# A hybrid layer and a mixture-of-experts block on one core: norms summed earlier and elsewhere, splits moved up, and down weights laid out as 8 KB rows

## The reference

```python
def hybrid_layer(x, ...):                       # block 1
    h = rmsnorm(x, ln1_g)
    z = h @ w_in                                # q, k, v of three attentions, conv input, forget gate, gates
    branches = (sliding_window_gqa, conformer_conv, forgetting_attention, moba_attention)
    merged = sum over branches of sigmoid(gate) * (branch @ w_br)
    x = x + merged @ w_out
    h2 = rmsnorm(x, ln2_g)
    u = causal_depthwise_conv(h2 @ w_up)        # D_FF = 2816
    return x + (silu(g_ff) * v_ff) @ w_down

def reference(...):
    x = rmsnorm(hybrid_layer(x), final_g)       # eps 1e-6
    h = rms_norm(x, attn_norm_g)                # block 2, eps 1e-5
    u_pool, u_q, u_k, u_v = split(h @ w_in_2)
    x = x + concat(multiscale_pool(u_pool), diff_attention(rotary(u_q), rotary(u_k), u_v)) @ w_out
    x = x + cross_attention(rms_norm(x, xattn_norm_g), rms_norm(mem, mem_norm_g), w_cq, w_ckv, w_co)
    x = x + moe_ffn(rms_norm(x, ffn_norm_g))    # 32 experts, top 4, clamped swiglu
    return rms_norm(x, final_norm_g)
```

## Time and profile before

| | before |
|---|---|
| time, median of 3 runs | 1783.1 us (1780.71 to 1783.13) |
| profiled execution | 1782.5 us, span 1780.7 us |
| PE busy | 1624.3 us, 91% of the span |
| DVE busy | 746.3 us, 42% |
| ACT busy | 485.1 us, 27% |
| POOL busy | 155.2 us, 9% |
| moved by DMA | 526.45 MB, mean 296 GB/s |

### The profile page before, as it was taken

One profiled execution on the slowest core, in us unless ns is written; L12 is line 12 of the kernel. 1 busy time (PEld: TensorE's weight loads), 2 busy tenths in 40 slices (PEclk: granted clock), 3 DMA queues, 4 the chain that ended last, 5 costly groups with the idle time before them and its releaser, 6 DMA issues.

```text
span 1780.7 us, 22817 instructions
## 1 busy us (share of the span) xinstructions
PE 1624.3 (91%) x9782; PEld 1030.0 (58%) x9782; DVE 746.3 (42%) x1308; ACT 485.1 (27%) x820; POOL 155.2 (9%) x190
## 2 busy tenths in 40 slices
PE   7899999989999899998999888898989898988885
PEld 6899989989999888985333323232323232323221
DVE  5798765778885567653211111111212121212122
ACT  3445645446554435542100000000101010101001
POOL 1200001403550012010000000000000000000000
PEclk9999999999999899999999999999999999999998
DMA  8564434546665353646899999999999999999995
GB/s 187 166 205 146 131 119 123 173 132 190 190 190 181 122 177 107 230 171 238 356 424 423 422 425 423 424 423 423 424 424 424 424 423 425 424 423 425 424 424 243
DMA packets 210938, 526.45 MB, mean 296 GB/s; under 512 B 18745, under 2 KB 136414, under 8 KB 178062
## 3 DMA queue, kind: packets, MB, share of 16 engines
q1 hardware_dynamic: 207104, 519.34, 75.6%
q0 software_dynamic: 3184, 5.37, 1.6%
q10 hardware_dynamic: 542, 0.21, 0.0%
HBM read 523.24 MB, written 1.61 MB: 295 GB/s over the span
## 4 chain that ended last, share of the span: by engine, by line
PE 56%; DMA 36%; DVE 5%; ACT 2%; issue 1%; SPq 0%; POOL 0%; ACTq 0%; DVEq 0%
PE bank L594 55%; DMA slot_ring<-in_w_down 13%; DMA slot_memx<-in_w_down 8%; DMA slot_late<-in_w_down 5%; DMA slot_high<-in_w_down 4%; DMA slot_late<-in_w_gu 2%; DVE slot_ring_r L1856 1%; DMA slot_last<-in_w_gu 1%; DMA slot_high<-in_w_gu 1%; DMA slot_ring<-in_w_in 1%; PE bank L1105 1%; ACT high_r L1441 0%; DVE rstd L1895 0%; DVE rot_tmp L2256 0%; DVE x_sb L1864 0%
## 5 line engine op out<-in xcount | busy, mean ns | idle before, releaser
L594 PE MATMUL bank<-h_hi_r,high_r 128*128 128x256 f32 x1000 | 286.4, 286 | 3.6 <-DVE h_lo_r L1856 3.6
L1856 DVE TENSOR_TENSOR slot_ring_r<-slot_ring,high_r 128x1024 fp32r<-128x1024 f32 x198 | 244.9, 1279 | 97.4 <-ACT high_r L1441 95.0
L594 PE MATMUL bank<-h_lo_r,high_r 128*128 128x256 f32 x1000 | 284.3, 284 | 0.0
L594 PE MATMUL bank<-h_hi_r,slot_ring_r 128*128 128x256 f32 x952 | 270.4, 284 | 0.0
L1860 DVE TENSOR_SCALAR ga<-bank 128x512 f32<-128x512 f32 x32 | 22.1, 692 | 583.8 <-PE bank L594 583.8
L1441 ACT ACTIVATE high_r<-slot_ring 128x1024 fp32r<-128x1024 f32 x198 | 198.0, 1052 | 73.0 <-PE bank L594 47.0
L594 PEld LDWEIGHTS bank<-h_hi_r,high_r 128*128 128x128 f32 x1000 | 192.1, 192 | 5.6 <-DVE h_lo_r L1856 4.3
L594 PEld LDWEIGHTS bank<-h_lo_r,high_r 128*128 128x128 f32 x1000 | 192.4, 192 | 0.1
L1441 ACT ACTIVATE th_e<-ga 128x512 f32<-128x512 f32 x32 | 20.2, 630 | 619.7 <-DVE ga L1860 619.7
L594 PEld LDWEIGHTS bank<-h_hi_r,slot_ring_r 128*128 128x128 f32 x952 | 183.4, 193 | 0.0
L594 PE MATMUL bank<-slot_ring,xg 128*64 128x512 f32 x528 | 124.3, 603 | 12.1 <-DMA slot_ring<-in_w_gu 12.1
(11 more groups left out here) (413 smaller groups left out, 2925.9 us busy)
## 6 DMA issues: line engine op xcount, KB each, us to landing
slot_ring<-in_w_gu SPq DMA_DIRECT2D x66, 1024.0 KB, 22.1
slot_high<-in_w_gu SPq DMA_DIRECT2D x50, 1024.0 KB, 22.1
slot_ring<-in_w_down SPq DMA_DIRECT2D x49, 1024.0 KB, 22.7
slot_last<-in_w_gu SPq DMA_DIRECT2D x38, 1024.0 KB, 22.2
slot_ring<-in_w_in SPq DMA_DIRECT2D x36, 1024.0 KB, 5.0
slot_late<-in_w_gu SPq DMA_DIRECT2D x32, 1024.0 KB, 22.1
slot_high<-in_w_down SPq DMA_DIRECT2D x25, 1024.0 KB, 23.3
slot_ring<-in_w_up SPq DMA_DIRECT2D x44, 512.0 KB, 4.6
```

The source lines that it names most:

```text
L594: return e.matmul(o, lhs, rhs, start=start, stop=stop, skip_group_check=True)
L1856: return e.tensor_tensor(o, i, j, op)
```

## The change

- **Start.** The first transfer of constants holds ident and ones only. The sums of squares come from x as it lands, token by token: eight DVE operations (128x256, `accum_out`), a reduction, ACT's root of two columns, a reciprocal, and two products with diag(norm) on PE that spread it over the partitions. The eight sums and squares and the wide reciprocal go. The rows are turned in two steps. h is split in halves with unit ub0's lo between them. The product for the bias tables comes after ub0 on PE, their copies after the split that goes with ub1 on DVE. The split of wfc moves ahead of the ub loop on ACT and behind it on DVE.
- **Memory's norm** goes in three steps of three, three and two tiles.
- **ln2, xattn, ffn.** `add_squares`: POOL adds tiles 2 and 3, then 4 and 5, of the squares to tiles 0 and 1; PE sums tiles 0, 1, 6 and 7 only, after the last projection.
- **Border.** The attn_g norm is computed straight from the residual: its squares are scaled by `gain_sq` = sqrt((g1^2 + eps2) / D), eps is eps1 * eps2, the gain is the product `gain12`. The squares for final_g follow on ACT into `x_sq`, POOL adds the eight tiles in three operations after the last rotation, PE needs one call, and DVE applies it between its splits for upool and the pooling. The mark that frees two more slots for SP comes at down's end.
- **Cross attention.** `cross_probs(2)` and `(3)` stand before `round_co(0)` and `(1)` on ACT.
- **Down units.** Partition p takes rows 2p and 2p+1, one row of 8 KB; the transposes read every other hidden column.

```diff
-        MEM_STEPS = ((0, 1), (2, 3), (4, 5), (6, 7), ())
+        MEM_STEPS = ((0, 1, 2), (3, 4, 5), (6, 7), (), ())
...
@@ tensor_program
-            for i in range(4):
-                sums("ln1_g", h, i)
...
+            turn_rows("cols", (0,))
+            banks.take(q, "token norms")
+            q.wait_ge(*dve["token norms"])
+            for t in range(TT):
+                m = matmul(bank("token norms")[:, t * P:(t + 1) * P], ones, mean_sb[:, t * P:(t + 1) * P], True, True)
...
+            turn_rows("more cols", (1, 2, 3))
             for c in range(BT):
                 project(("ub", c), hs, h_of("ln1_g"), (dve, ("glu", c)))
+                if c == 0:
+                    matmul(bank("diag0")..., relb[:, 0:SWA_H], diag_const..., True, True)
...
             def add_residual(w, src, ready, norm):
                 for i in range(4):
                     project((w, i), src, ready, (dve, ("residual", w, i)))
-                    if i:
-                        sums(norm, h, i - 1)
+                sums(norm, h, 0)
                 sums(norm, h, 3)
...
-            pe.mark("final start")
-            for i in range(4):
-                sums("final_g", h, i)
+            pe.mark("block2")
             memory_unit(2)
-            pe.mark("block2")
             for i in range(4):
                 sums("attn_g", h, i)
             memory_unit(3)
...
+                if i == 0:                      # between upool 0 and 1
+                    q.wait_ge(*pool["squares", "final_g"])
+                    matmul(bank(("final_g", "sums"))[:, 0:S], ones, x_sq[:, 0, :], True, True)
...
                 for j in range(4):
-                    m = e.transpose(b_down[:, j * P:(j + 1) * P], upv[:, j * P:(j + 1) * P], ident)
+                    pair = upv[:, j // 2 * 256:(j // 2 + 1) * 256].rearrange("p (n k) -> p n k", k=2)
+                    m = e.transpose(b_down[:, j * P:(j + 1) * P], pair[:, :, j % 2], ident)
@@ sync_program
-            e.dma_start(const_sb[:, 0:4 * P], a["consts"][:, 0:4 * P])
+            e.dma_start(const_sb[:, 0:2 * P], a["consts"][:, 0:2 * P])
...
-  load_dn(q, n - 1, u, w_dn[n - 1, u * 256:(u + 1) * 256, :].rearrange("(k p) n -> p k n", p=P))
+  load_dn(q, n - 1, u, w_dn[n - 1, u * 256:(u + 1) * 256, :].rearrange("(p k) n -> p k n", p=P))
@@ POOL
+            def add_squares(norm):              # at ln2, xattn and ffn start
+                for i in (1, 2):
+                    e.tensor_tensor(h[:, 0:2, :], h[:, 0:2, :], h[:, 2 * i:2 * i + 2, :], ALU.add)
...
+            q.wait_ge(*act["square", "final_g", 3])
+            q.wait_ge(*pe["rot", "uk", BT - 1])
+            for n in (4, 2, 1):
+                e.tensor_tensor(x_sq[:, 0:n, :], x_sq[:, 0:n, :], x_sq[:, n:2 * n, :], ALU.add)
             q.wait_ge(*dve["pool zero"])
@@ ACT
+            af(token_norm, token_norm, ACT.Sqrt, bias=eps_col[EPS1])
...
+            sqrt_table()                        # block2
+            for i in range(4):
+                q.wait_ge(*dve["residual", "down", i])
+                for k in (2 * i, 2 * i + 1):
+                    af(h[:, k, :], x[:, k, :], ACT.Square, scale=gain_sq[:, k:k + 1])
+            memory_unit(2)
+            root("attn_g", EPS1 * EPS2, "ln2_g")
             round_h("attn_g")
             memory_unit(3)
+            for i in range(4):
+                squares("final_g", x_sq, x, i, dve["residual", "down", i])
...
+            cross_probs(2)
+            cross_probs(3)
             round_co(0)
             round_co(1)
-            cross_probs(2)
-            cross_probs(3)
@@ DVE
+            for i in range(4):
+                q.wait_ge(*x_ins[i]["x"])
+                for t in range(TT):
+                    piece = xin[:, t, i * 256:(i + 1) * 256]
+                    e.scalar_tensor_tensor(out=h[:, TT * i + t, :], in0=piece, scalar=1.0 / D, in1=piece, op0=ALU.mult, op1=ALU.mult,
+                                           accum_out=token_sums[:, t, i:i + 1])
...
+            for half in range(2):
+                (four h of ln1_g; four lo of h; rest(("ub", 0), half), a half of the unit's lo)
...
+                for i in range(2 if c == 1 else 0):
+                    q.wait_ge(*pe["diag"])
+                    e.tensor_copy(diag_sb[i], ...)
...
+            q.wait_ge(*act["wfc hi"])           # behind the ub loop, before: behind qa's
+            tt(wfc_s.lo, wfc, wfc_s.hi, ALU.subtract)
...
-            apply("final_g", x, x)
             memory_unit(2)
-            apply("attn_g", x, h, hs.lo)
+            apply("attn_g", x, h, hs.lo, gain=gain12)
             memory_unit(3)
...
             for i in range(2):
                 ahead(("upool", i))
+            apply("final_g", x, x)
             for t in two:
                 e.memset(t[:, 0:16], 0.0)
```

More of the change, by code:

```diff
@@ L617, in sums @@
                 q.wait_ge(*sq_by(norm, i)["square", norm, i])
+                if norm in ADDED:
+                    q.wait_ge(*pool["squares", norm])
                 for k in (2 * i, 2 * i + 1):
@@ L679, in tensor_program, with turn_rows @@
[L679 to L687, removed]
+            def turn_rows(name, groups):
+                banks.take(q, name)
+                for t in groups:
+                    r = n_rows[t]
+                    q.wait_ge(*rows_ins[t]["rows"])
+                    m = e.transpose(bank(name)[:, t * P:t * P + r], rows_sb[0:r, t * P:(t + 1) * P], ident[0:r, 0:r])
+                m.then_inc(*pe.step(name))
+                banks.give(name, (dve, name))
@@ L1478, in root, with round_h @@
                 af(rstd, bank((norm, "sums"))[:, 0:S], ACT.Sqrt, bias=eps_col[eps]).then_inc(*act.step("root", norm))
-            def round_h(norm, dst=None):
-                for k in range(KT):
+            def round_h(norm, blocks=range(KT)):
+                for k in blocks:
                     q.wait_ge(*dve["h", norm, k])
@@ new lines, in vector_program, with columns_of @@
+            own()
+            e.tensor_reduce(token_norm, token_sums, AX.X, ALU.add).then_inc(*dve.step("token squares"))
+            evac(("x", 2), x[:, 4:6, :], two_of(("x", 2)), ("x", 2))
+            q.wait_ge(*act["token roots"])
+            e.reciprocal(token_norm, token_norm).then_inc(*dve.step())
+            own()
+            for t in range(TT):
+                ts(mean_sb[:, t * P:(t + 1) * P], ident, token_norm[:, t:t + 1], ALU.mult).then_inc(*dve.step("token norms"))
+            def columns_of(name, groups):
+                q.wait_ge(*pe[name])
+                for t in groups:
+                    r = n_rows[t]
+                    e.tensor_copy(cols_sb[:, t * P:t * P + r], bank(name)[:, t * P:t * P + r]).then_inc(*dve.step(name))
@@ new lines, in vector_program @@
+            columns_of("cols", (0,))
+            evac(("token rows",), rstd, bank("token norms")[:, 0:S], ("token norms",))
+            own()
+            split_done[0] = 1
+            for half in range(2):
+                for k in range(4 * half, 4 * half + 4):
+                    q.wait_ge(*(act if k // 2 % 2 else dve)["x", k // 2])
+                    stt(h[:, k, :], x[:, k, :], col("ln1_g", k), rstd, ALU.mult, ALU.mult).then_inc(*dve.step("h", "ln1_g", k))
+                for k in range(4 * half, 4 * half + 4):
+                    q.wait_ge(*act["h hi", "ln1_g", k])
+                    tt(hs.lo[:, k, :], h[:, k, :], hs.hi[:, k, :], ALU.subtract).then_inc(*dve.step("h split", "ln1_g", k))
+                rest(("ub", 0), half)
```

134 lines of the change are left out of this document (74 added, 60 removed).

## The result

The changed kernel takes 1754.4 us (median of 4 runs, 1752.54 to 1756.71), before 1781.9 in the same comparison; the ratio is 0.9849, interval 0.9836 to 0.9861. Run once more beside the experiments it took 1750.7 us, ratio 0.9821 (0.9807 to 0.9836). The forecast was 1754.9. The profiled execution took 1753.4 us, its span is 1751.6. One of the six runs of e12, 1986.2 us at a granted clock of 0.75, is a slow one and is left out of its row in the table of the experiments.

What follows compares the result with a forecast made beforehand. PE was taken as the bound until about 846 us, the experts' weight loads at full DMA rate after. Terms -6.4 - 0.6 - 4.1 - 14.7 + 3.5 - 3.3 - 2.0 = -27.6 gave 1754.9 us, range 1744 to 1765.

Steps and rivals of the forecast that it cites:

- The likeliest case: Whole kernel: the terms' sum of -27.6 us holds, giving 1754.9 us, within 1750 to 1760; chance 0.55.
- The start, -6.4: To 110 us: earlier norm and wfc split save 6.4 us, as the tables' block still delays units; bounds 4.5 and 12.7.
- Memory's steps, -0.6: Memory's norm in three steps for four: wait for memn's lo ends, 0.6 us saved; bounds -1.5 and +2.5.
- Sums of four tiles, -4.1: ln2, xattn, ffn: PE drops two groups of sums each, POOL adds instead; 1.6, 1.6 and 0.9 us saved.
- The border, -14.7 and +3.5: Between the blocks: PE sums once without waits, 14.7 us saved; final norm's work in the diff attention costs 3.5 back.
- Cross, -3.3: Cross attention: ps first on ACT removes PE's 2.87 us wait and some 0.4 of slow products; bounds -1.5 and -4.0.
- Rows, -2.0: Experts' loads: down's units as 8 KB rows save 2.0 us, from 0 to 2.6 by pairs of windows.
- Transposes, hidden: Experts: strided transposes, four in 0.59 us, stay hidden because PE idles 25 of 200 us there.
- B: Start: queues share, so the bias tables' transfers don't hold units up; start gives 12.7 us, total 1748.6; chance 0.15.
- C: Experts' loads: the 8 KB rows pay their upper bound, 10.9 us instead of 2.0, total 1746.0; chance 0.10.
- D: Work taken off PE returns on DVE: final norm costs 7.8 us, memory and cross gains vanish, total 1763.1; chance 0.15.
- E: Experts: slow strided transposes make PE the bound, gains lost from 5.2 us an expert, 1809 at 6 us; chance 0.03.

Runs made afterwards that it cites:

- e12: Changed kernel with the final norm's eight tiles summed by PE and POOL's three additions gone; 1754.1 us, ratio to before 0.9845.
- e7: Changed kernel with both POOL transfers of the bias tables held until PE has ended the sixth unit; 1746.5 us, ratio to before 0.9806.
- e5: Changed kernel with the split of wfc moved back behind qa's conv steps on ACT and DVE; 1758.5 us, ratio to before 0.9872.
- e11: Changed kernel with ACT's old order in the cross attention, roundings of mix ahead of the copies to ps; 1754.4 us, ratio to before 0.9835.
- e10: Changed kernel with eight tiles summed on PE again for ln2, xattn and ffn, without POOL's additions there; 1757.0 us, ratio to before 0.9859.
- e8: Changed kernel with the border of the blocks as before, final norm first and then the attention norm; 1763.8 us, ratio to before 0.9901.
- e3: Changed kernel with the final norm's eight apply products moved between the diff attention's heads on DVE; 1751.2 us, ratio to before 0.9830.
- e1: Kernel before with only the down units as 8 KB rows and the transposes that go with them; 1779.2 us, ratio to before 0.9974.

## Why the prediction was right, and where it was off

The likeliest case held, the total within 0.5 us, but that is partly luck: PE brought the experts 28.5 us forward where 25.6 were forecast, the rows gave about 5 where 2.0 were, and the profile's end took 4.6 back that the forecast didn't have. One of the prediction's own signs of being wrong, that the experts' stretch changes by more than 4 us, did come true (4.2 to 5.4). The term that failed is the one for the rows; the mechanisms of the others held, with the sizes below.

- **The start, -6.4:** -6.6 measured; with the spread of the eight profiles it is 5.3 to 7.8, so that it hit within 0.2 is luck. The step that said that the tables' block moves along and eats the gain of the norm is shown by e7 (block away: 3.9 us more in the profile) and e5 (wfc's wait back: nothing left). What the step left out is the stretch at half clock behind wfc's wait, which goes with it (e5). PE began 1.3 us later than forecast, for ACT rounds h ahead of hi, and it did not matter: e11 begins at 19.0 and has its 312th product at 85.7, as the changed kernel, which begins at 20.3.
- **Between 150 us and ln2:** -1.6 us nobody forecast. One stretch of half clock is missing in the profile of the changed kernel: before has 48 products of a unit in 7.4 us from 151.50, after in 5.9 from 144.92. The second profile of the changed kernel has such a stretch at 146 us, and from the 312th product to the last units of the branches the fourteen profiles take 250.2 to 252.6 us, with before's 252.1 and the changed kernel's 250.5 among them. Chance, then, not the change.
- **Memory's steps, -0.6:** about -0.3 by the two profiles, as waits of 3.6 us for lo took the place of the 4.4; no kernel had it alone.
- **Sums of four tiles, -4.1:** 4.3 to 4.8 by e10; the loss to POOL's bias operations was mis-sized.
- **The border, -14.7 and +3.5:** -14.9 and +2.9 in the profiles (by the prediction's own bounds, down's end to the second unit's end, -14.2); e8 confirms the whole. The sum of what comes back is near, its parts are not: 1.4 was counted for POOL's additions and 1.2 for the apply, and together they cost PE 0.9 (e3, e12), although DVE's steps were stretched by 2.9; ACT's squares, counted at 0.9, cost about 1.2 by the chain, and 0.6 within uq0 was not forecast.
- **Cross, -3.3:** -3.4 (e11). The slow products gave 1.4 where 0.4 was counted, and 0.7 of the wait's 2.9 was left or came back.
- **Rows, -2.0:** mis-sized: 4.2 to 5. The window of before that was read as mostly down's (1009 to 1026 us) has the landings of seven units, of which two are down's; its 0.5%, put on two units and not on four, is 0.04 each and some 5 us in all, as an estimate. Going from 2.6 to 2.0 for the pair of windows with 421 each made the miss larger. A kernel with the rows alone gives the price in one window.
- **Transposes, hidden:** right, 0.67 us for 0.59, PE still idles.
- **Rivals:** B's turns show in one window, and its effect isn't there; C's 10.9 is out; D's contention stretches DVE by 2.9 us, and at most 0.9 of it reaches PE; E is out, for it needed 5.2 us where the transposes take 0.67.
- **The end:** the forecast had nothing for it. 1.7 us belong to the changed kernel, 2.9 came and went with the clock.

## What to carry to other kernels

When a stall at the head of a pipeline is shortened, look for what holds the next units: here 10 us of transfers in 4.6 KB packets stood in the way of the weights, and by the profiles holding them back until the pipeline had slack gave 3.9 us, where the earlier start by itself gave nothing (e7, e5). Work taken off the bound engine is cheap on an idle one even where the two slow each other (e12), as long as the delayed steps lie beside the bound engine's. And a layout change that moves a rate by half a per cent is read from one window of the steady stretch in a kernel that has only this change, not from windows inside one trace, unless the units that land in each are counted.

## What the runs showed that was not expected

- In one window of the changed kernel two queues' packets passed about one for one: with 4.6 KB packets from 8 partitions on one and 256-byte packets on the other, 58 packets took 94.1% of the engines and 71 took 1.6%. In before's window it was 199 to 1.
- Down units in packets of 8 KB instead of 4 (16,385 packets fewer) raise the rate from 424 to 426 GB/s.
- GpSimd additions of 1024 and 512 columns beside DVE stretch single DVE operations of 0.42 us to 2.19 and 1.52; without the additions (e12) they take 0.42.
- A DVE product with two fp32 sources and a running sum takes 0.35 us from one to the next, no longer than one without (0.40).
- All twelve profiles of the changed program and its variants have 1.4 to 2.0 us more between the last landing and the end than before and e1 have (clock aside), cause open; the granted clock falls in PE's last expert in two of the twelve, at a cost of 2.9 us.
